# Later first gates, norm sums and row transposes, six weight blocks' high parts on ACT, mLSTM outputs in halves

## The reference

```
layer 0:  x += concat(y_a, attention) @ w_out        from one projection of rmsnorm(x)
            u -> causal conv -> r, i = sigmoid gates; log_a = -8 r softplus(-lambda)
            h_t = a h_(t-1) + sqrt(1-a^2) (i u);  y_a = h * gelu(g)
            attention: windows of 128 keys, ALiBi, sinks
layer 1:  x += h @ c_w_out                           mLSTM, 4 heads of 256
            u -> conv -> silu -> q, k ; v, o and two gates per head from the projection
            chunkwise matrix memory; h = layernorm(sigmoid(o) * num / norm) * norm_g
each:     x += (silu(gate) * up) @ w_down            of rmsnorm(x), hidden width 2816
          x += sigmoid(x @ w_g) * (p @ w_p)          "ple"
final rmsnorm; caches and states are outputs too
```

## Time and profile before

| | |
|---|---|
| median of 3 runs | 2821.64 us (2818.73 to 2822.49) |
| profiled execution | 2819.4 us, its span 2817.6 us |
| PE busy | 2719.1 us, 97% |
| DVE / ACT / POOL busy | 1471.2 / 598.3 / 950.1 us |
| POOL: one high part (L477) / one low part (L479), means | 2.03 / 2.55 us |
| matmuls of `hilo` on 128 x 352 | 0.33 us each, overlapping, 13464 of them |
| mean granted TensorE clock | 0.984 |

### The profile page before, as it was taken

How to read it: one execution, slowest core, us unless ns; L and a number is a source line. 1 busy time by engine, 2 the same in 40 slices (tenths; PEclk the granted TensorE clock), 3 DMA queues, 4 the chain that set the end, 5 groups by cost and what they waited for, 6 DMA issues and landing times.

```text
span 2817.6 us, 40938 instructions
## 1 busy us (share of the span) xinstructions
PE 2719.1 (97%) x17224; PEld 2671.0 (95%) x17224; DVE 1471.2 (52%) x2331; ACT 598.3 (21%) x1262; POOL 950.1 (34%) x439
## 2 busy tenths in 40 slices
PE   7899999999999999998999999899999999999996
PEld 7798899999999999998999988799999999999996
DVE  7956475444444444657754046646444444444565
ACT  3434331000000000133122146422000000000042
POOL 4222044433333333333424310024333333333430
PEclk9999999999999999999999999999999999999998
DMA  4101011111111111113122231311111111111111
GB/s 143 37 23 61 32 61 46 45 46 46 48 49 46 46 45 47 51 46 116 45 83 91 85 102 54 122 31 60 46 45 46 45 45 46 45 46 45 53 38 62
DMA packets 57831, 160.10 MB, mean 57 GB/s; under 512 B 7340, under 2 KB 28332, under 8 KB 56368
## 3 DMA queue, kind: packets, MB, share of 16 engines
q1 hardware_dynamic: 31056, 109.79, 12.7%
q10 hardware_dynamic: 26592, 47.70, 4.7%
HBM read 137.07 MB, written 20.40 MB: 56 GB/s over the span
## 4 chain that ended last, share of the span: by engine, by line
PE 90%; DVE 7%; ACT 2%; issue 1%; DMA 0%; ACTq 0%; DVEq 0%
PE ps L426 28%; PE ps L427 28%; PE ps L428 28%; PE ps L635 1%; PE ps L605 1%; PE ps L836 1%; DVE xl L1483 1%; DVE xl L938 1%; DVE uc L1209 1%; PE ps L852 1%; PE ps L871 1%; DVE cs L1501 1%; DVE hb L1547 0%; PE ps L617 0%; PE ps L842 0%
## 5 line engine op out<-in xcount | busy, mean ns | idle before, releaser
L426 PE MATMUL ps<-xh,wh 128*128 128x352 f32 x3432 | 1122.6, 327 | 28.5 <-DVE xl L938 14.4
L427 PE MATMUL ps<-xl,wh 128*128 128x352 f32 x3432 | 1114.7, 325 | 0.0
L428 PE MATMUL ps<-xh,wl 128*128 128x352 f32 x3432 | 1114.0, 325 | 0.0
L477 POOL TENSOR_TENSOR wh<-raw,seeds 128x1024 fp32r<-128x1024 f32 x208 | 422.3, 2030 | 1782.7 <-PE ps L428 1754.4
L426 PEld LDWEIGHTS ps<-xh,wh 128*128 128x128 f32 x3432 | 651.8, 190 | 33.7 <-issue 13.9
L427 PEld LDWEIGHTS ps<-xl,wh 128*128 128x128 f32 x3432 | 651.9, 190 | 2.1 <-issue 0.2
L428 PEld LDWEIGHTS ps<-xh,wl 128*128 128x128 f32 x3432 | 652.0, 190 | 0.0
L479 POOL TENSOR_TENSOR wl<-raw,wh 128x1024 fp32r<-128x1024 f32 x208 | 529.7, 2547 | 16.3
L1054 DVE TENSOR_TENSOR tmpa<-ps,rstd 128x352 f32<-128x352 f32 x132 | 69.1, 524 | 719.1 <-PE ps L428 711.0
L426 PE MATMUL ps<-hh,wh 128*128 128x352 f32 x1056 | 340.4, 322 | 0.0
L428 PE MATMUL ps<-hh,wl 128*128 128x352 f32 x1056 | 340.0, 322 | 0.0
(11 more groups left out here) (264 smaller groups left out, 2478.1 us busy)
## 6 DMA issues: line engine op xcount, KB each, us to landing
raw<-wstream SPq DMA_DIRECT2D x208, 512.0 KB, 3.6
vod<-stage ACTq DMA_DIRECT2D x72, 128.0 KB, 1.9
vb<-vod ACTq DMA_DIRECT2D x9, 512.0 KB, 4.0
ob<-vod ACTq DMA_DIRECT2D x9, 512.0 KB, 3.8
x<-xT ACTq DMA_DIRECT2D x3, 1408.0 KB, 12.4
x<-xT ACTq DMA_DIRECT2D x2, 2112.0 KB, 7.4
xsave<-x ACTq DMA_DIRECT2D x1, 4224.0 KB, 11.5
x<-xsave ACTq DMA_DIRECT2D x1, 4224.0 KB, 13.1
```

Source lines behind the costliest of these rows:

```text
L426: pe.matmul(out, whi, mhi, start=first, stop=False)
L427: pe.matmul(out, whi, mlo, start=False, stop=False)
L428: return pe.matmul(out, wlo, mhi, start=False, stop=last)
L477: pool.tensor_tensor(hi, raw[:, r, :], zero, ALU.add).then_inc(hi_made, 1)
```

## The change

- The first gates run after unit 12 instead of 11; before each of the four gate groups ACT does a sigmoid of one column. POOL holds block 6 back until the first convolution is done.
- `transpose_v` alternates between banks 6 and 7; only the ninth transpose waits for the first copy.
- ACT makes the high parts of six blocks (the first two of each FFN, the gate block and the first U block), within the tail phases at units 20 and 21; POOL makes only their low parts. The first U block's low part waits for two thirds of `xl`, the second U block for all of it.
- After "gate0" none of the norm sums runs inside the tail; all three follow the gate block, and roots and reciprocals with them.
- The rows' transposes run after the third unit of the V projection.
- `out_high` and `out_low` count each half of four feature tiles; the query matmuls wait half by half.
- "out1" runs units (0,0) (0,1) (1,0) (1,1) (0,2) (1,2) first; its start no longer waits for the last but one chunk's `out_low`, the last transposes stay behind two units and do, and the wait for the last `out_low` stands before the fifth unit.

```diff
+        ACT_HIGH = [b for b0 in (B0_FFN, B1_GATE, B1_FFN) for b in (b0, b0 + 1)]
...
+        TAIL["out1"] = [(0, 0), (0, 1), (1, 0), (1, 1), (0, 2), (1, 2)] + by_block[6:] + last_half
...
-            later = {B0_FFN + 2: "ffn0", B1_FFN + 2: "ffn1"}
+            later = {B0_FFN + 2: XLN["ffn0"] + KT * NT, B1_FFN + 2: XLN["ffn1"] + KT * NT,
+                     B1_GATE + 1: XLN["mix1"] + KT * 2, B1_GATE + 2: XLN["mix1"] + KT * NT}
...
                 if b in later:
-                    pool.wait_ge(xl_ready, 1 + XLN[later[b]] + KT * NT)
+                    pool.wait_ge(xl_ready, 1 + later[b])
+                if b == 6:
+                    pool.wait_ge(uc_ready, 1)
...
+                if b in ACT_HIGH:
+                    pool.wait_ge(high_made, ACT_HIGH.index(b) + 1)
+                else:
+                    pool.tensor_tensor(hi, raw[:, r, :], zero, ALU.add).then_inc(hi_made, 1)
+                    pool.wait_ge(hi_made, b + 1 - sum(a < b for a in ACT_HIGH))
...
                     if last_chunk is not None and u == 2:
+                        pe.wait_ge(cl_ready, 1 + 2 * (CH - 1))
                         transpose_h(last_chunk)
-                        pe.wait_ge(cl_ready, 1 + CH)
+                    if last_chunk is not None and u == 4:
+                        pe.wait_ge(cl_ready, 1 + 2 * CH)
...
-                    if u == first or u == first + 4:
+                    if ni != 2 and u in (first, first + 4):
                         norm_sum(ni, (u - first) // 4)
...
-                    if j == 4:
+                    if j == 8:
                         pe.wait_ge(v_ready, 1)
-                    if j == 8:
-                        pe.wait_ge(v_ready, 2)
-                    mm = pe.transpose(ps[0:n, 7, (j % 4) * P:(j % 4 + 1) * P], vt[:, j * P:j * P + n], ident[:, :])
+                    mm = pe.transpose(ps[0:n, 6 + j // 4 % 2, (j % 4) * P:(j % 4 + 1) * P], vt[:, j * P:j * P + n], ident[:, :])
...
-                if u in (11, 14, 17):
-                    lru_gates((11, 14, 17).index(u))
+                if u in (12, 14, 17):
+                    lru_gates((12, 14, 17).index(u))
...
-            dense(B1_GATE % NW, B1_GATE, FREE0["g1"] - 6, OFF["g1"], XLN["mix1"], 2)
+            dense(B1_GATE % NW, B1_GATE, FREE0["g1"] - 6, OFF["g1"], XLN["mix1"])
+            for tt in range(NT):
+                norm_sum(2, tt)
...
                         for j in range(CH):
+                            if pair == 0 and j == 3:
+                                rows_to_columns()
...
-                    if w == 0 and n > 0:
-                        pe.wait_ge(cl_ready, n)
                     for t in range(KT):
+                        if w == 0 and n >= 2 and t % 4 == 0:
+
+                            pe.wait_ge(cl_ready, 1 + 2 * (n - 2) + t // 4 + 1)
...
-            pe.wait_ge(cl_ready, CH)
+            pe.wait_ge(cl_ready, 1 + 2 * (CH - 2))
...
-                        if u == 20:
+                        if u == 20 and ni != 2:
                             rstd_of(ni, 0)
...
-                    rstd_of(ni, 1)
-                    rstd_of(ni, 2)
+                    for tt in range(0 if ni == 2 else 1, NT):
+                        rstd_of(ni, tt)
...
-                dve.wait_ge(ch_ready, n + 1)
                 for t in range(KT):
+                    if t % 4 == 0:
+                        dve.wait_ge(ch_ready, 2 * n + t // 4 + 1)
...
-                    if t < KT - 1:
+                    if t % 4 < 3:
                         step.mark(ins)
...
+            def weight_high(b):
+
+                act.wait_ge(raw_landed[b % NRAW], 16 * (b // NRAW + 1))
+                act.wait_ge(block_done, b + 1)
+                act.activation(wh[:, b % NW, :, :].rearrange("p k c -> p (k c)"), raw[:, b % NRAW, :],
+                               ACT.Copy).then_inc(high_made, 1)
...
+                if ni < 4 and u in (20, 21):
+                    weight_high((B0_FFN, B1_GATE, B1_FFN)[ni - 1] + u - 20)
...
-                    if u == 19 or u == 23:
+                    if ni != 2 and u in (19, 23):
                         root(ni, (u - 19) // 4)
...
-                        root(ni, 2)
+                        for tt in range(0 if ni == 2 else 2, NT):
+                            root(ni, tt)
...
             def gates(t):
+                act.activation(seeds[:, 7:8], seeds[:, 0:1], ACT.Sigmoid)
...
                     ins = act.activation(xh[:, t, ds(col, width)], ps[:, 6 + t // 4, (t % 4) * P:(t % 4) * P + width],
                                          ACT.Copy, scale=vec("c_g", t))
-                ins.then_inc(ch_ready, 1)
+                    if t % 4 == 3:
+                        ins.then_inc(ch_ready, 1)
```

More of the change, by code:

```diff
@@ L209, in build @@
         hi_made = sem("hi_made")
+        high_made = sem("high_made")
+        ACT_HIGH = [b for b0 in (B0_FFN, B1_GATE, B1_FFN) for b in (b0, b0 + 1)]
         zero_ready = sem("zero_ready")
@@ L345, in build @@
         TAIL = {"out0": by_tile + last_half}
-        for name in ("gate0", "out1", "gate1"):
+        for name in ("gate0", "gate1"):
             TAIL[name] = by_block + last_half
+        TAIL["out1"] = [(0, 0), (0, 1), (1, 0), (1, 1), (0, 2), (1, 2)] + by_block[6:] + last_half
         SKIP = {"out0": 8, "gate0": 0, "out1": 0, "gate1": 0}
@@ L522, in tail_phase, with dense @@
                     first = 18 if ni < 4 else 17
-                    if u == first or u == first + 4:
+                    if ni != 2 and u in (first, first + 4):
                         norm_sum(ni, (u - first) // 4)
-            def dense(slot, b, free, bank0, xl_at=None, sums=None):
+            def dense(slot, b, free, bank0, xl_at=None):
                 pe.wait_ge(raw_free, split_count(b))
                 for tt in range(NT):
-                    if tt == 1 and sums is not None:
-                        norm_sum(sums, NT - 1)
                     pe.wait_ge(acc_free, free + tt + 1)
@@ L772, in _ @@
                     norm_sum(0, (3, 6, 9).index(u))
-                if u == 11:
+                if u == 12:
                     pe.wait_ge(m0_in, 16 * 5)
-                if u in (11, 14, 17):
-                    lru_gates((11, 14, 17).index(u))
+                if u in (12, 14, 17):
+                    lru_gates((12, 14, 17).index(u))
                 if u == 20:
@@ L786, in _, with rows_to_columns @@
             ple(0, B0_PLE)
-            dense(B1_GATE % NW, B1_GATE, FREE0["g1"] - 6, OFF["g1"], XLN["mix1"], 2)
+            dense(B1_GATE % NW, B1_GATE, FREE0["g1"] - 6, OFF["g1"], XLN["mix1"])
+            for tt in range(NT):
+                norm_sum(2, tt)
             dense_loop("u1", B1_U, KT)
[L791 to L804, removed]
+            def rows_to_columns():
+                pe.wait_ge(rows_ready, 1)
+                pe.wait_ge(c_in, 16 * 4)
+                for cc in range(CH):
+                    for q in range(4):
+                        r = (0, 5, 4, 1)[q]
+                        pe.transpose(ps[:, 6, (cc * 4 + q) * 4:(cc * 4 + q + 1) * 4],
+                                     rows[:, r, cc * P:(cc + 1) * P], ident[0:4, 0:4])
+                for h in range(H):
+                    mm = pe.matmul(ps[:, 6, 256 + CH * h:256 + CH * (h + 1)], sel[:, h, :], rsmall[:, 32:32 + CH],
+                                   start=True, stop=True)
+                for cc in range(CH):
+                    n = P if cc < CH - 1 else TS
+                    mm = pe.transpose(ps[0:n, 6, 320 + 4 * cc:324 + 4 * cc], rstd[0:4, cc * P:cc * P + n], ident[0:4, 0:4])
+                mm.then_inc(cols_done, 1)
             for half in range(2):
@@ L1788, in values @@
                 if j < 2:
-                    act.activation(vtok[:, 4 * j + 1:4 * j + 5, :].rearrange("p a d -> p (a d)"), ps[:, 7, :],
+                    act.activation(vtok[:, 4 * j + 1:4 * j + 5, :].rearrange("p a d -> p (a d)"), ps[:, 6 + j, :],
                                    ACT.Copy).then_inc(v_ready, 1)
                 else:
-                    act.activation(vtok[0:TS, 10, :], ps[0:TS, 7, 0:P], ACT.Copy).then_inc(v_ready, 1)
+                    act.activation(vtok[0:TS, 10, :], ps[0:TS, 6, 0:P], ACT.Copy).then_inc(v_ready, 1)
             gates(0)
@@ L2043, in _ @@
             act.dma_start(O["c_o"][0], cs[:, :, :, :]).then_inc(c_sent, 16)
-            act.wait_ge(cl_ready, 1 + CH)
+            act.wait_ge(cl_ready, 1 + 2 * CH)
             act.wait_ge(c_sent, 32)
```

2 lines of the change are left out of this document (removed).

## The result

The changed kernel takes 2777.9 us (median of four runs, 2777.0 to 2779.3), the kernel before 2820.8 (four runs, 2818.7 to 2822.5): a ratio of 0.9849, with a 95% interval of 0.9832 to 0.9866. The profiled execution took 2779.3 us, its span 2777.5, at a mean granted clock of 0.990. Two later executions were slow ones, one of the experiment e1_log1p_early (7816 us) and one of the kernel before (3859 us), and are in no ratio or median here.

The account below looks back on a forecast made before the run. PE, busy 97% of the span, was taken as the bound, leaving pauses and half clock to win. Six parts sum to 44.1 us: 2819.4 profiled becomes 2775.3, plus 2.2 for the median 2777.5 us; range 2768 to 2794.

Parts of the forecast that it names:

- Part 1: First gates and value transposes: the first pause mostly moves to the second gates; 3.0 us won, bounds 0 and 9.
- Rival (b): First gates: log1p not held up, 9 us won instead of 3, other bounds high; time 2768 us; chance 0.07.
- Part 2: Start of the first FFN: high parts on ACT let DVE free PE's bank sooner; 0.8 us, bounds 0 and 1.4.
- Part 3: Layer 1's first norm and gate block: PE's 9.8 us wait for the last sum goes; 9.1 us, bounds 5.5 and 10.5.
- the new wait of 1.8 us at the third sum: After the gate block: PE's third norm matmul waits for ACT's first root, table load included, 1.8 us.
- Part 4: Rows' transposes inside the V projection: 4.7 us wait and 6.2 us of half-clock loss go; 10.9 us, bounds 4.7 and 10.9.
- Half clock in the V projection: V projection: a sign named beforehand that would show the prediction wrong; no size given.
- rival (a): Norm, rows and last projection: half clock stays after pauses and among light matmuls; sum 29.2, time 2792.4 us; chance 0.16.
- Part 5: mLSTM outputs in halves: query matmuls end 1.03 us earlier in six chunks, plus 0.7; 6.9 us, bounds 3.5 and 9.6.
- Part 6: Last projection, four units around the last transposes: waits of 3.8 and 4.5 us and half clock go; 13.4 us, bound 8.3.
- (c): Whole kernel: little happens, bank waits the same behind other releasers; under 5.6 us won; chance 0.02.
- (d): Two FFNs: PE without pauses loses full clock; 100 us at half clock gives 2827 us; chance 0.03.

Follow-up runs that it names:

- e1_log1p_early: a3 with log1p moved before the input norm's first reciprocal and the second convolution before the first product: 2769.2 us, median of five, ratio 0.9814 to the kernel before.
- a1: Changed kernel without POOL holding block 6 back: 2783.1 us in one run, its start 3.7 us late.
- a2: Changed kernel with POOL holding block 6 back until log1p is done, instead of the first convolution: 2777.0 us.
- a4: Changed kernel with the first gates after unit 11 again, block 6 still held back: 2783.5 us, its start 3.9 us late.
- a3: Changed kernel with ACT also making the high parts of blocks 6 to 10: 2770.2 us, median of four, ratio 0.9828 to the kernel before.
- b2: Changed kernel with POOL making all high parts again: 2780.1 us.
- f1: Changed kernel without POOL's two new waits before the low parts of the first two U blocks: 2791.3 us in one run, 4.2 us of it a late start.
- b1: Changed kernel with norm sums, roots and reciprocals of layer 1's first norm back in their old places: 2777.4 us.
- c1: Changed kernel with the rows' transposes back between the U and the V projection: 2786.1 us.
- d1: Changed kernel with the query matmuls waiting for both halves of out_low at once: 2781.5 us.
- d2: Changed kernel with the wait for the last out_low back behind two units instead of four in the last projection: 2777.3 us.

## Why the prediction was right, and where its terms were not

**Total.** 2777.5 us were predicted, 2777.9 measured. The sum was better than its terms: they add up to 44.1 us, the two spans differ by 40.1. The prediction put the median 2.2 us above the profiled execution, as it was before; after the change the profiled one happens to lie 1.4 us above the median. These 3.6 us are luck, and they cover most of the 4.0 that the sum was too large.

**Part 1** (3.0, measured 4.0). The steps went as written: log1p held up by POOL, the product at 78.20 (78.6 forecast), the pause moved to the second gates, a single wait in the transposes. Off in size was the second convolution: it ended at 85.8, not 88.5. Block 8 came at 81.79, when one of the three steps had run; POOL's instructions were the longer ones here (2.87 and 3.25 us), and DVE's only 1.5 us slower together. The third convolution was then 1.4 us early, not level, and this is the 1.0 us more. The starts of the same PE instructions divide the part: the third gates come 1.4 us earlier (106.04, 104.65), where the forecast had 0.3 from DVE; with the value transposes behind them it is 2.75 (133.40, 130.65), and behind the fourth gates 4.0 (146.42, 142.40). The last two steps, 1.35 and 1.3 us, are near the 1.35 and 1.4 that the forecast gave to the second bank and the early sigmoid; no run takes either of these out, so which of them won what is read from the timelines, not shown. The runs a1, a2, a4 and a3 show the rule behind DVE's part: the attention starts within 0.6 us of the same time while the number of POOL instructions beside DVE's chain stays the same, and 7.2 us come as soon as five of these go. Rival (b), log1p not held up and 9 us won, didn't come true, and its way to the prize is closed: in a2 log1p ran free and the attention started 0.6 us later. The Trainium skill's lock ("SBUF — State Buffer", section "Who interferes with whom") agrees with every row above, down to operations on 4 elements.

**Part 2** (0.8, measured 0.8). Right, and b2 shows that it is the high parts on ACT.

**Part 3** (9.1, measured 11.2). The cause was right, POOL beside DVE; f1 gives 8.2 us to two waits of POOL alone, b2 1.4 to the high parts, b1 nothing to the order of the sums; the other 1.6 us they don't explain singly. The step that failed is the new wait of 1.8 us at the third sum. It counted ACT's table load behind the first sum. The timeline of ACT in the changed kernel shows it ahead of the sum, in idle time:

```profile
1303.84 1.28 ACT L1622 ACT_TABLE_LOAD   x1
1309.06 0.55 ACT L1622 ACTIVATE rt<-ps,vecs 128x352 f32<-128x352 f32 x1 [3.94 <-PE ps L513]
```

The load started 4.4 us before the sum's matmul (1308.27), and only the square root waited; PE pauses 0.15 us. That is 1.65 of the 2.1 us above the forecast.

**Part 4** (10.9, measured 8.65). The wait of 4.7 went as said. The half clock didn't go altogether: it lasts 3.4 us, right behind the rows' small transposes, and 1.5 us stay lost, for f1, the one run without this dip, is 1.5 us faster from the V projection's start to the first keys (210.1 us for 211.6). "Half clock in the V projection" was named as what would show the prediction wrong; in this part it is. It is rival (a)'s mechanism, on a small scale. The other 0.7 us are less than the 1.3 us by which c1, with the rows in their old place, and the kernel before differ in this stretch (7.3 and 8.65 us above the changed kernel).

**Part 5** (6.9, measured 5.96). A chunk won 0.89 us (18.77 to 17.88), not 1.03. The forecast took four steps and four matmuls off as one; the rows show the wait go from 1.48 to 0.45, which is the 1.03, and the eight matmuls of the queries stretch from 2.05 to 2.19 us, since the second four wait as well:

```profile
1684.55 2.19 PE L853 MATMUL ps<-uu,cbd 128*128 128x128 f32 x16 [0.45 <-DVE xl L1501]
```

**Part 6** (13.4, measured 11.5). The second wait went, and 3.6 of the 3.8 us of the first. What failed is again "no half clock": 3.4 us of it are left at the start. In a2, c1 and d1, which have the same code there and no such dip, the stretch from the projection's start to the last norm is 1.5 us shorter (986.0 us for 987.5), so 1.5 us is its price. The row shows what is left of the first wait:

```profile
1773.85 0.40 PE L431 MATMUL ps<-xh,wh 128*128 128x352 f32 x1 [2.13 <-issue]
```

**Not in the sum at all:** the U projection became 1.55 us slower (last section).

**Rivals.** (a) came true in single dips, worth 3.0 us in parts 4 and 6 together, not in part 3. Both dips came in some executions and not in others of the same code. (c) and (d) didn't: the first FFN ran its 760 us at 1.00 with 760.00 us busy.

## What to carry to other kernels

When two engines take turns, moving one's work about moves the pause; count the instructions of the one that lie in the other's critical stretch, and take some away, by a third engine (five high parts on ACT: 7.2 us) or by a wait that puts them into the other's idle time (two waits: 8.2 us). In a sum of removed pauses, allow for one short dip of half clock (3.4 us here, worth 1.5) wherever light matmuls remain, and look for small work, such as a log1p on 4 elements, that could run where nobody contends. And judge a part by its own milestones: the same stage differed by 7 us between executions of the same code.

## What the runs showed of the hardware that was not expected

**Matmul spacing.** In the U projection the matmuls start every 159.5 ns in the kernel before, and every 161.7 ns after, in the same order and at full clock. The windows have it as instruction counts: 349 in 56 us above, and before the change, in the same part of the projection,

```profile
1334.00:1390.00 56.00, 56.00 (x354) 56.00 (x353) 52.03 (x32) 9.83 (x23) 29.24 (x10) 1.00 0.13 39
```

Both spacings occur in both kernels elsewhere, the faster in the second FFN's start (159.4 ns over 80 us), the slower in all tail phases. All eleven experiments have 161.7 in the U projection, also those that put back the order of the sums (b1), POOL's high parts (b2) and the timing of its low parts (f1). None of these is the cause. One experiment does change the spacing, in another place: in d2 the last projection's tail runs at 159.2 ns, in all others at 161.7, and the only edit is where PE waits. A pause there isn't enough by itself either, since the kernel before paused 4.5 us at the same place and ran at 161.7 behind it. What sets the spacing stays open. It accounts for 576 x 2.2 ns = 1.3 of the 1.55 us that the U projection lost. It is worth knowing: 2.2 ns on each of 10,000 matmuls are 22 us.

**Short dips of half clock.** A dip of 3.4 us follows the rows' small transposes with no pause of PE (1416.2); with the transposes there, it came in the changed kernel and in nine of ten experiments (in b2 for 6.8 us), and not in f1. Two other dips come and go between executions of the same code: in the program's first 30 us, where PE pauses for 1.1 to 1.9 us at a time, in six of the eleven experiments and not in the changed kernel's execution; and at the start of the last projection, missing in a2, c1 and d1, in d2 later, at the wait.

**What POOL doesn't hold up.** DVE's operations with a source in PSUM, and its RECIPROCAL, took their usual time beside POOL. In the changed kernel the add `x<-ps,x` (L1098) took 0.51 us in the median where it started beside a POOL instruction (247 times) and 0.53 elsewhere, and the reciprocal of 128x352 2.35 us either way. The product `tmpb<-tmpb,tmpa` (L1050), with both sources in SBUF, took 1.44 us beside POOL (88 times) and 0.52 elsewhere.
